# Expert weights fetched through two hardware queues instead of one, from block 56 on

## The chip, the cores and the metric

The program runs on one core of a Trainium2 chip. The metric is the device time in microseconds (us) of one execution. TensorE (PE) does the matrix products, VectorE (DVE) and ScalarE (ACT) the elementwise work, GpSimd (POOL) little here, and SyncE (SP) only issues transfers. A transfer that SyncE or ScalarE issues goes into that engine's own hardware queue; the queues are worked off by the core's 16 DMA engines.

## The reference, cut to what matters

Two transformer blocks run one after the other over 512 tokens of width 1024. The first ends in an expert layer: each of 16 experts takes its 64 best tokens, and everything is float32.

```
aff = softmax(h @ w_router); gate, idx = top_k(aff^T, 64)
xs = h[idx]                                          # per expert 64 x 1024
hid = silu(xs @ w_gate[e]) * (xs @ w_up[e])          # w_gate, w_up: 16 x 1024 x 2048
ys = (hid @ w_down[e]) * gate                        # w_down: 16 x 2048 x 1024
```

The three weights of the 16 experts are 403 MB of the 526 MB that the kernel reads.

## The kernel before, in words

The expert stage handles two experts at a time, in 8 passes p = 0 to 7. Expert 2p uses columns 0 to 63 of TensorE's array, expert 2p + 1 columns 64 to 127, so their matmuls alternate. The weights come in 192 blocks of 2048 KB, 24 to a pass. Block n has p = n // 24 and r = n % 24; even r is the even expert's, odd r the odd one's. r = 0 to 7 are the gate weights (four pairs), 8 to 15 the up weights, 16 to 23 the down weights. In what follows "pair m" is the blocks m and m + 1 with m even; TensorE starts on a pair when both blocks have landed (`landed_block`, line 1060).

In a pass TensorE does the four gate pairs (line 1075) with the combining of the pass before between them (line 1049), the four up pairs with the gathering of the next pass's tokens (line 1032), then the turning of h (`turn_h`, with VectorE's product of line 2448 and ScalarE's copies around it), and the four down pairs (line 1142).

From block 46 on there are 8 slots for weights in SBUF, and block n goes to the slot that block n - 8 had (`SLOT_OF`, `BEFORE`). `moe_used(BEFORE[n])` is the semaphore value that TensorE sets when it has used that block's pair. SyncE's program (`sync`) issues all blocks in order of n: for each it waits for `moe_used`, then issues line 540. The last four blocks, 188 to 191, are issued in halves and quarters (lines 543 and 548), so that the last matmuls wait for little.

ScalarE's loop over p (line 1722) does, for each pass: wait for the gate pairs, four Silu (line 1727); the four copies of hT; wait for the last down pair, two copies to ys.

Of the kernel before, what the change touches and what calls it, by code (L numbers as in the profile page):

```python
# [12 lines left out]
P = 128  # L13
# [31 lines left out]
def build_program(nc, I, out):  # L45
    ctx = ExitStack()
    with ctx:
        s = {n: ctx.enter_context(nc.semaphore("s_" + n)) for n in DMA_SEMS + SEMS}
# [5 lines left out]
        def up(ins, name, *key):  # L54
            ins.then_inc(s[name], 1)
            count[name] = at[(name, *key)] = at[name] = count.get(name, 0) + 1
# [4 lines left out]
        def val(name, *key):  # L61
            return at.get((name, *key) if key else name, 1) if counting else at[(name, *key) if key else name]
# [17 lines left out]
        def mem(n, at_=None):  # L80
            if at_ is None:
                at_ = cursor[0]
                cursor[0] += n
            assert at_ + n <= NW, (at_, n)
            assert at_ + n <= M or at_ >= M
            return low[:, at_:at_ + n] if at_ < M else high[:, at_ - M:at_ - M + n]
# [6 lines left out]
        def own(n, at_):  # L93
            if (at_, n) not in full:
                full[at_, n] = lay(f"f_{at_}_{n}", at_, n, F32)
            return full[at_, n][:, :]

        def v3(ap, a):
            return ap.rearrange("p (a b) -> p a b", a=a)

        def flat(ap):
            return ap.rearrange("p a b -> p (a b)")
# [72 lines left out]
        NBLK = 192  # L175
        HALVES = {10: (10, 11), 12: (12, 13), 14: (14, 16), 17: (17,), 18: (18, 19)}
        HALVED = [n for pair_ in HALVES.values() for n in pair_]
        moe_slot = [own(4096, a_) for a_ in (M + 20096, M + 24192, 0, 4096, M + 16000, 8192, 12288, XT_AT, M + 28288)]
        once_x, once_y, once_z = own(4096, M + 8704), own(3072, M + 12800), own(1024, M + 5120)
        turn_of = [8, 0, 1, 2, 3, 4, 5, 6, 7]  # L180
        SLOT_OF, FILLED, BEFORE, held = {}, {}, {}, {}
        for n in range(NBLK):
            if n in (7, 15):
                continue
            if n == 46:
                turn_of.remove(7)
            i = SLOT_OF[n] = turn_of[0]
            turn_of = turn_of[1:] + [i]
            BEFORE[n] = held.get(i)
            FILLED[n] = FILLED.get(held.get(i), 0) + (2 if n in HALVED else 1)  # L190
            held[i] = n
        ys = mem(1024, M + 12800)
        stm = v3(mem(2048, M + 13824), 4)
        sq2 = [mem(512, M + 24704), mem(512, M + 25216)]
# [237 lines left out]
        offk = [0, 512, 896, 1152]  # L432


        def sync(sp):
            def load_chunk(c):
                for i, (dst, src) in enumerate(chunks[c][0](whole(c))):
                    sp.dma_start(dst, src).then_inc(s[{ZF: f"zf{i}", CG: f"cg{i}"}.get(c, f"w{pair[c]}")], 16)
# [51 lines left out]
            sp.wait_ge(s[freed(N1 - 3)[0]], val(*freed(N1 - 3)))  # L490
            load_chunk(N1 - 1)

            def block(n):
                p, r = divmod(n, 24)
                e = 2 * p + r % 2
                if r < 16:
                    k = r % 8 // 2
                    src = I["w_up" if r > 7 else "w_gate"][0, e][256 * k:256 * k + 256, :]
                    return src.rearrange("(p r) n -> p (r n)", p=P)
                k = (r - 16) // 2  # L500
                return I["w_down"][0, e][512 * k:512 * k + 512, :].rearrange("(p r) n -> p (r n)", p=P)

            for n in (0, 1, 2, 15, *range(3, 15), *range(16, NBLK)):
                if n == 1:
                    sp.wait_ge(s["pe_inter"], val("pe_inter", 1, 3))
                    sp.wait_ge(s["a_fill"], val("a_fill"))
                    sp.wait_ge(s["v_fill"], val("v_fill"))
                    sp.wait_ge(s["g_y"], val("g_y"))
                    for i in range(2):
                        sp.dma_start(xres[:, 2 * i:2 * i + 2, :], x_v[:, 2 * i:2 * i + 2, :]).then_inc(s[f"x{i}"], 16)  # L510
                r, src = n % 24, block(n)
                k = (r - 16) // 2
                if n == 15:
                    sp.wait_ge(s["v_mix"], val("v_mix", "on", 3))
                    sp.wait_ge(s["pe_mix"], val("pe_mix", "xr", 3, 1))
                    sp.dma_start(once_x, src).then_inc(s["mx"], 16)
                    continue
                if n == 7:
                    sp.dma_start(once_y, src[:, 0:3072]).then_inc(s["my"], 16)
                    sp.dma_start(once_z, src[:, 3072:4096]).then_inc(s["my"], 16)  # L520
                    continue
                if n in HALVED:
                    for half, z in enumerate((slice(0, 2048), slice(2048, 4096))):
                        for m in HALVES.get(n, ()):
                            used = moe_used(BEFORE[m]) if half else half_used(BEFORE[m])
                            sp.wait_ge(s[used[0]], val(*used))
                            sp.dma_start(moe_slot[SLOT_OF[m]][:, z], block(m)[:, z]).then_inc(s[f"m{SLOT_OF[m]}"], 16)
                    continue
                i = SLOT_OF[n]
                if BEFORE[n] is not None:  # L530
                    used = moe_used(BEFORE[n])
                    sp.wait_ge(s[used[0]], val(*used))
                elif n == 9:
                    sp.wait_ge(s["pe_route"], val("pe_route", "h2", 3, 1))
                elif n == 3:
                    sp.wait_ge(s["pe_mix"], val("pe_mix", "res", 3))
                elif n == 5:
                    sp.wait_ge(s["pe_mix"], val("pe_mix", "res", 7))
                if n < NBLK - 4:
                    sp.dma_start(moe_slot[i], src).then_inc(s[f"m{i}"], 16)  # L540
                    continue

                sp.dma_start(moe_slot[i][:, 0:2048], src[:, 0:2048]).then_inc(s[f"m{i}"], 16)
                if r % 2:
                    for name, c0, c1 in (("mg", 2048, 4096),) if k == 2 else (("mh", 2048, 3072), ("mq", 3072, 4096)):
                        for e_ in range(2):
                            src = I["w_down"][0, 14 + e_][512 * k:512 * k + 512, :].rearrange("(p r) n -> p (r n)", p=P)
                            sp.dma_start(moe_slot[SLOT_OF[n - 1 + e_]][:, c0:c1], src[:, c0:c1]).then_inc(s[f"{name}{e_}"], 16)
# [21 lines left out]
        def half_used(n):  # L570
            return ("pe_half", n // 8, n % 8 // 2)

        def moe_used(n):

            p, r = divmod(n // 2, 12)
            return ("pe_down", p, r - 8) if r >= 8 else ("pe_up", p, r // 4, r % 4)
# [918 lines left out]
        def scalar(a):  # L1495
            def bank(*key):
                return banks[bank_of[key]] if key in bank_of else banks[0]

            def copy(o, i):
                return a.activation(o, i, ACT.Copy)  # L1500
# [194 lines left out]
            for t in range(4):  # L1695
                z = slice(128 * t, 128 * t + 128)
# [22 lines left out]
                                    scale=rtok[:, t:t + 1]), "a_route", "h2", t, half)  # L1719


            for p in range(8):
                a.wait_ge(s["pe_up"], val("pe_up", p, 0, 3))
                if p:
                    a.wait_ge(s["v_up"], val("v_up", p - 1, 3))
                for fc in range(4):
                    up(a.activation(stm[:, fc, :], bank("up", p, 0, fc)[:, :], ACT.Silu), "a_up", p, fc)  # L1727
                if p:
                    a.wait_ge(s["pe_down"], val("pe_down", p - 1, 3))
                if p == 1:  # L1730
                    for j in range(8):
                        a.wait_ge(s["pe_back"], val("pe_back", j))
                        up(copy(XT[:, j, :], bank("back", j)[:, :]), "xt_back", j)
                for fc in range(4):
                    a.wait_ge(s["pe_up"], val("pe_up", "h", p, fc))
                    up(copy(flat(hT[:, 4 * fc:4 * fc + 4, :]), bank("hT", p, fc)[:, :]), "hT", p, fc)
                a.wait_ge(s["pe_down"], val("pe_down", p, 3))
                if p:
                    a.wait_ge(s["pe_comb"], val("pe_comb", p - 1, 7))
                if p == 7:  # L1740
                    up(copy(ys[:, 0:128], bank("y", p, 0)[:, 0:128]), "ys", p, "first")
                    up(copy(ys[:, 128:512], bank("y", p, 0)[:, 128:512]), "ys", p, 0)
                    continue
                for f in range(2):
                    up(copy(ys[:, 512 * f:512 * f + 512], bank("y", p, f)[:, :]), "ys", p, f)
# [1242 lines left out]
        counting = False  # L2988
        block = ctx.enter_context(nc.Block())
        block.sync(sync)  # L2990
        block.scalar(scalar)
        block.vector(vector)
        block.gpsimd(gpsimd)
# [26 lines left out]
```

## Time and profile before

| | |
|---|---|
| median of 3 runs | 2102.88 us (2102.07 to 2102.92) |
| profiled execution | 2102.45 us |
| its span, first to last instruction | 2100.7 us |
| TensorE busy | 2007.0 us (96%) |
| VectorE, ScalarE busy | 907.5 us, 577.4 us |
| DMA | 529.60 MB, mean 252 GB/s |
| expert stage | about 394 to 1302 us of the span |

The profile's page gives busy time by engine, the span in 40 slices of 52.5 us, and the chain of waits that ended last. TensorE's busy time includes time in which it runs at less than its peak, so 96% does not say by itself that TensorE bounds every stage; the slices of DMA and the chain have to be read with it.

### The profile page before, as it was taken

To read this page: it belongs to the slowest core of one execution; us is meant where nothing else is said; L and a number is where in the kernel's file an instruction comes from. 1 tells how busy PE (TensorE), PEld (TensorE's weight loads), DVE (VectorE), ACT (ScalarE), POOL (GpSimd) and SP (SyncE) were. 2 spreads that over 40 slices of the span, in tenths; PEclk is the share of its full clock that TensorE was granted. 3 is DMA by queue.
4 is the path that set the end of the run, shared out by engine and by line. 5 is a ranking of instruction groups with operands and counts; after the bars stand their busy time and mean duration, and the time that the engine had idled before them with its cause. 6 is when DMAs were issued, how large, how long until landed. Compare 5 with 4: busy or idle time off the path is not lost.

```text
span 2100.7 us, 23813 instructions
## 1 busy us (share of the span) xinstructions
PE 2007.0 (96%) x9908; PEld 1254.4 (60%) x9908; DVE 907.5 (43%) x1489; ACT 577.4 (27%) x901; POOL 59.0 (3%) x107
## 2 busy tenths in 40 slices
PE   7999999999999999999999889999999999999998
PEld 5888777543533333242423324776788888888886
DVE  4666673320111111111101002777897566666555
ACT  5434323100100000000000001438635343344445
POOL 1000010000000000000000000005200000000000
PEclk9999999999999999999999999999999999999999
DMA  9462117898999999999999998142122322323222
GB/s 350 160 236 85 41 67 295 353 404 371 431 430 430 431 430 430 432 430 431 430 431 430 431 431 363 63 121 41 67 94 81 131 80 95 106 80 111 81 97 84
DMA packets 109228, 529.60 MB, mean 252 GB/s; under 512 B 15189, under 2 KB 43969, under 8 KB 83137
## 3 DMA queue, kind: packets, MB, share of 16 engines
q1 hardware_dynamic: 109121, 528.07, 62.3%
q8 instruction: 80, 1.31, 0.2%
q14 instruction: 27, 0.22, 0.0%
HBM read 525.95 MB, written 2.10 MB: 251 GB/s over the span
## 4 chain that ended last, share of the span: by engine, by line
PE 86%; DMA 7%; DVE 4%; issue 2%; ACT 1%; SPq 0%; POOL 0%; ACTq 0%; DVEq 0%
PE bank L1075 22%; PE bank L640 14%; PE bank L642 14%; PE bank L641 14%; DMA f<-in_w_gate_dram 6%; PE bank L1142 6%; PE bank L1032 3%; PE bank L1049 3%; PE bank L651 2%; PE bank L1241 1%; PE bank L1350 1%; DMA f<-in_w_in_dram 1%; DMA high<-in_x_dram 1%; PE bank L867 1%; DVE r L407 0%
## 5 line engine op out<-in xcount | busy, mean ns | idle before, releaser
L1075 PE MATMUL bank<-f,high 128*64 128x512 f32 x2048 | 473.1, 610 | 36.8 <-issue 18.1
L640 PE MATMUL bank<-r 128*128 128x512 f32 (+1 forms) x984 | 388.7, 395 | 3.4 <-DVE r L2084 2.7
L641 PE MATMUL bank<-r 128*128 128x512 f32 (+1 forms) x984 | 384.0, 390 | 0.0
L642 PE MATMUL bank<-r 128*128 128x512 f32 (+1 forms) x984 | 384.0, 390 | 0.0
L1075 PEld LDWEIGHTS bank<-f,high 128*64 128x64 f32 x2048 | 150.4, 139 | 328.7 <-issue 313.6
L1142 PE MATMUL bank<-f,high 128*64 128x512 f32 x1024 | 227.7, 603 | 7.7 <-issue 7.6
L1500 ACT ACTIVATE high<-bank 128x512 f32<-128x512 f32 (+3 forms) x97 | 53.2, 579 | 636.0 <-PE bank L651 296.8
L2419 DVE SCALAR_TENSOR_TENSOR f<-bank,low,f 128x512 f32<-128x512 f32 x64 | 48.0, 750 | 398.6 <-PE bank L1049 398.1
L640 PEld LDWEIGHTS bank<-r 128*128 128x128 f32 (+1 forms) x984 | 184.5, 187 | 48.4 <-issue 5.8
L642 PEld LDWEIGHTS bank<-r 128*128 128x128 f32 (+1 forms) x984 | 184.4, 187 | 40.0
L641 PEld LDWEIGHTS bank<-r 128*128 128x128 f32 (+1 forms) x984 | 184.5, 188 | 39.0 <-issue 0.7
L407 DVE TENSOR_TENSOR r<-f,r 128x1024 fp32r<-128x1024 f32 (+3 forms) x171 | 193.5, 1184 | 31.9 <-ACT r L401 31.8
L401 ACT ACTIVATE r<-f 128x1024 fp32r<-128x1024 f32 (+3 forms) x172 | 163.6, 1016 | 24.8 <-DMA f<-in_w_in_dram 10.2
L1142 PEld LDWEIGHTS bank<-f,high 128*64 128x64 f32 x1024 | 76.0, 139 | 153.5 <-issue 153.5
L640 PE MATMUL bank<-r,r 128*128 128x512 f32 (+1 forms) x400 | 150.2, 375 | 0.0
L642 PE MATMUL bank<-r,r 128*128 128x512 f32 (+1 forms) x400 | 149.0, 372 | 0.0
L641 PE MATMUL bank<-r,r 128*128 128x512 f32 (+1 forms) x400 | 148.9, 372 | 0.0
L2405 DVE TENSOR_SCALAR high<-bank,low 128x128 f32<-128x128 f32 x64 | 25.6, 406 | 279.0 <-PE bank L1032 279.0
L1727 ACT ACTIVATE high<-bank 128x512 f32<-128x512 f32 x32 | 16.5, 602 | 296.3 <-PE bank L1075 296.3
L640 PEld LDWEIGHTS bank<-r,r 128*128 128x128 f32 x400 | 75.4, 188 | 15.8 <-issue 2.0
L642 PEld LDWEIGHTS bank<-r,r 128*128 128x128 f32 x400 | 75.4, 188 | 13.2
L641 PEld LDWEIGHTS bank<-r,r 128*128 128x128 f32 x400 | 75.4, 189 | 12.8
(377 smaller groups left out, 1798.7 us busy)
## 6 DMA issues: line engine op xcount, KB each, us to landing
f<-in_w_gate_dram SPq DMA_DIRECT2D x63, 2048.0 KB, 23.4
f<-in_w_down_dram SPq DMA_DIRECT2D x60, 2048.0 KB, 26.3
f<-in_w_up_dram SPq DMA_DIRECT2D x59, 2048.0 KB, 25.6
f<-in_w_up_dram SPq DMA_DIRECT2D x32, 1024.0 KB, 7.3
f<-in_w_in_dram SPq DMA_DIRECT2D x13, 2048.0 KB, 7.7
high<-in_w_ada_dram SPq DMA_DIRECT2D x32, 512.0 KB, 5.4
f<-in_w_down_dram SPq DMA_DIRECT2D x14, 1024.0 KB, 10.5
f<-in_w_ada_dram SPq DMA_DIRECT2D x4, 2048.0 KB, 14.6
```

What stands on the lines that cost most here:

```text
L401: up(a.activation(high_part(c)[:, z], whole(c)[:, z], ACT.Copy), "hi", c, i)
L407: up(v.tensor_tensor(low_part(c)[:, z], whole(c)[:, z], high_part(c)[:, z].bitcast(F32), ALU.subtract), "lo_v", c, i)
L640: pe.matmul(o, wh, xh, start=first, stop=False)
L641: pe.matmul(o, wl, xh, start=False, stop=False)
L642: return pe.matmul(o, wh, xl, start=False, stop=last)
L651: ins = pe.transpose(o[:, m * n:m * n + m] if k == P else o[:, k * n:k * n + k], b, ident[0:k, 0:k])
L1032: ins = pe.matmul(o, H2[:, t, 256 * (k // 2) + k % 2:256 * (k // 2) + 256:2], Sp[i][:, t, :], start=t == 0, stop=t == 3)
L1049: up(pe.matmul(o[:, :], ys[:, 128 * d:128 * d + 128], SgT[p % 2], start=True, stop=True), "pe_comb", p, d)
L1075: ins = pe.matmul(o[64 * e:64 * e + 64, :], xsT[p % 2][:, 2 * k + r, 64 * e:64 * e + 64], ws[e](2048 * r + 512 * fc), start=k == 0 and r = ...
L1142: ins = pe.matmul(o[f][64 * e:64 * e + 64, :], hT[:, 4 * k + r, 64 * e:64 * e + 64], ws[e](1024 * r + 512 * f), start=k + r == 0, stop=k = ...
L1500: return a.activation(o, i, ACT.Copy)
L2419: up(v.scalar_tensor_tensor(out=XT[:, d, :], in0=bank("cb", p, d)[:, :], scalar=adaT[:, 40 + d, 0:1], in1=XT[:, d, :], op0=ALU.mult, op1=A ...
```

## The change

From block 56 on, the odd blocks up to 187 are issued by ScalarE; the even ones, and the blocks 188 to 191, stay with SyncE. ScalarE issues them in `refills(p, r0)`, called at three places of a pass, each time for the slots that the pairs of the next part free. The waits are the same values of the same semaphores.

```diff
--- before.py
+++ after.py
@@ -189,6 +189,10 @@
             BEFORE[n] = held.get(i)
             FILLED[n] = FILLED.get(held.get(i), 0) + (2 if n in HALVED else 1)
             held[i] = n
+        by_act = {}
+        for n in range(56, NBLK - 4):
+            if n % 2:
+                by_act.setdefault(BEFORE[n], []).append(n)
         ys = mem(1024, M + 12800)
         stm = v3(mem(2048, M + 13824), 4)
         sq2 = [mem(512, M + 24704), mem(512, M + 25216)]
@@ -432,6 +436,16 @@
         offk = [0, 512, 896, 1152]
 
 
+        def expert_block(n):
+            p, r = divmod(n, 24)
+            e = 2 * p + r % 2
+            if r < 16:
+                k = r % 8 // 2
+                src = I["w_up" if r > 7 else "w_gate"][0, e][256 * k:256 * k + 256, :]
+                return src.rearrange("(p r) n -> p (r n)", p=P)
+            k = (r - 16) // 2
+            return I["w_down"][0, e][512 * k:512 * k + 512, :].rearrange("(p r) n -> p (r n)", p=P)
+
         def sync(sp):
             def load_chunk(c):
                 for i, (dst, src) in enumerate(chunks[c][0](whole(c))):
@@ -490,16 +504,6 @@
             sp.wait_ge(s[freed(N1 - 3)[0]], val(*freed(N1 - 3)))
             load_chunk(N1 - 1)
 
-            def block(n):
-                p, r = divmod(n, 24)
-                e = 2 * p + r % 2
-                if r < 16:
-                    k = r % 8 // 2
-                    src = I["w_up" if r > 7 else "w_gate"][0, e][256 * k:256 * k + 256, :]
-                    return src.rearrange("(p r) n -> p (r n)", p=P)
-                k = (r - 16) // 2
-                return I["w_down"][0, e][512 * k:512 * k + 512, :].rearrange("(p r) n -> p (r n)", p=P)
-
             for n in (0, 1, 2, 15, *range(3, 15), *range(16, NBLK)):
                 if n == 1:
                     sp.wait_ge(s["pe_inter"], val("pe_inter", 1, 3))
@@ -508,7 +512,7 @@
                     sp.wait_ge(s["g_y"], val("g_y"))
                     for i in range(2):
                         sp.dma_start(xres[:, 2 * i:2 * i + 2, :], x_v[:, 2 * i:2 * i + 2, :]).then_inc(s[f"x{i}"], 16)
-                r, src = n % 24, block(n)
+                r, src = n % 24, expert_block(n)
                 k = (r - 16) // 2
                 if n == 15:
                     sp.wait_ge(s["v_mix"], val("v_mix", "on", 3))
@@ -519,12 +523,14 @@
                     sp.dma_start(once_y, src[:, 0:3072]).then_inc(s["my"], 16)
                     sp.dma_start(once_z, src[:, 3072:4096]).then_inc(s["my"], 16)
                     continue
+                if n > 55 and n % 2 and n < NBLK - 4:
+                    continue
                 if n in HALVED:
                     for half, z in enumerate((slice(0, 2048), slice(2048, 4096))):
                         for m in HALVES.get(n, ()):
                             used = moe_used(BEFORE[m]) if half else half_used(BEFORE[m])
                             sp.wait_ge(s[used[0]], val(*used))
-                            sp.dma_start(moe_slot[SLOT_OF[m]][:, z], block(m)[:, z]).then_inc(s[f"m{SLOT_OF[m]}"], 16)
+                            sp.dma_start(moe_slot[SLOT_OF[m]][:, z], expert_block(m)[:, z]).then_inc(s[f"m{SLOT_OF[m]}"], 16)
                     continue
                 i = SLOT_OF[n]
                 if BEFORE[n] is not None:
@@ -1719,12 +1725,21 @@
                                     scale=rtok[:, t:t + 1]), "a_route", "h2", t, half)
 
 
+            def refills(p, r0):
+                for r in range(r0, r0 + 8):
+                    for n in by_act.get(24 * p + r, ()):
+                        used = moe_used(BEFORE[n])
+                        a.wait_ge(s[used[0]], val(*used))
+                        a.dma_start(moe_slot[SLOT_OF[n]], expert_block(n)).then_inc(s[f"m{SLOT_OF[n]}"], 16)
+
             for p in range(8):
+                refills(p, 0)
                 a.wait_ge(s["pe_up"], val("pe_up", p, 0, 3))
                 if p:
                     a.wait_ge(s["v_up"], val("v_up", p - 1, 3))
                 for fc in range(4):
                     up(a.activation(stm[:, fc, :], bank("up", p, 0, fc)[:, :], ACT.Silu), "a_up", p, fc)
+                refills(p, 8)
                 if p:
                     a.wait_ge(s["pe_down"], val("pe_down", p - 1, 3))
                 if p == 1:
@@ -1734,6 +1749,7 @@
                 for fc in range(4):
                     a.wait_ge(s["pe_up"], val("pe_up", "h", p, fc))
                     up(copy(flat(hT[:, 4 * fc:4 * fc + 4, :]), bank("hT", p, fc)[:, :]), "hT", p, fc)
+                refills(p, 16)
                 a.wait_ge(s["pe_down"], val("pe_down", p, 3))
                 if p:
                     a.wait_ge(s["pe_comb"], val("pe_comb", p - 1, 7))
```

On SyncE, where the up weights of pass 2 are issued (blocks 56 on; the number behind f_ is the slot's place, and 44928 stands for block 55), the kernel before has:

```order
L540 DMA f_44928_4096<-in_w_gate_dram 128x4096 [waits s_pe_down]
L540 DMA f_49024_4096<-in_w_up_dram 128x4096 [waits s_pe_up]
L540 DMA f_0_4096<-in_w_up_dram 128x4096 [waits s_pe_up]
L540 DMA f_4096_4096<-in_w_up_dram 128x4096 [waits s_pe_up]
L540 DMA f_40832_4096<-in_w_up_dram 128x4096 [waits s_pe_up]
L540 DMA f_8192_4096<-in_w_up_dram 128x4096 [waits s_pe_up]
L540 DMA f_12288_4096<-in_w_up_dram 128x4096 [waits s_pe_up]
L540 DMA f_53120_4096<-in_w_up_dram 128x4096 [waits s_pe_up]
```

and the changed kernel has:

```order
L546 DMA f_44928_4096<-in_w_gate_dram 128x4096 [waits s_pe_down]
L546 DMA f_49024_4096<-in_w_up_dram 128x4096 [waits s_pe_up]
L546 DMA f_4096_4096<-in_w_up_dram 128x4096 [waits s_pe_up]
L546 DMA f_8192_4096<-in_w_up_dram 128x4096 [waits s_pe_up]
L546 DMA f_53120_4096<-in_w_up_dram 128x4096 [waits s_pe_up]
```

The rows with slots 0, 40832, 12288 and 44928 behind block 55, the odd blocks, are gone from SyncE; an even block now follows an even block.

On ScalarE, the kernel before has around passes 2 and 3 (L1500 are copies to hT and ys, L1727 the Silu):

```order
L1500 ACTIVATE high<-bank 128x512 [waits s_pe_comb,s_pe_down]
L1500 ACTIVATE high<-bank 128x512
L1727 ACTIVATE high<-bank 128x512 [waits s_v_up,s_pe_up]
L1727 ACTIVATE high<-bank 128x512 x3
L1500 ACTIVATE high<-bank 128x512 [waits s_pe_up,s_pe_down]
L1500 ACTIVATE high<-bank 128x512 [waits s_pe_up] x3
L1500 ACTIVATE high<-bank 128x512 [waits s_pe_comb,s_pe_down]
L1500 ACTIVATE high<-bank 128x512
```

and the changed kernel has (L1506 and L1741 are the same copies and Silu, L1733 the new transfers):

```order
L1506 ACTIVATE high<-bank 128x512 [waits s_pe_comb,s_pe_down]
L1506 ACTIVATE high<-bank 128x512
L1733 DMA f_4096<-in_w_up_dram 128x4096 [waits s_pe_up] x4
L1741 ACTIVATE high<-bank 128x512 [waits s_v_up,s_pe_up]
L1741 ACTIVATE high<-bank 128x512 x3
L1733 DMA f_4096<-in_w_down_dram 128x4096 [waits s_pe_up] x4
L1506 ACTIVATE high<-bank 128x512 [waits s_pe_up,s_pe_down]
L1506 ACTIVATE high<-bank 128x512 [waits s_pe_up] x3
L1733 DMA f_4096<-in_w_gate_dram 128x4096 [waits s_pe_down] x4
L1506 ACTIVATE high<-bank 128x512 [waits s_pe_comb,s_pe_down]
L1506 ACTIVATE high<-bank 128x512
```

Four transfers, each behind its own wait for TensorE, now stand ahead of the Silu, ahead of the hT copies and ahead of the ys copies of each pass.

## Rows read from the trace of the kernel before

**Rows 1.** Page, the span in 40 slices, GB/s moved by DMA
```profile
GB/s 350 160 236 85 41 67 295 353 404 371 431 430 430 431 430 430 432 430 431 430 431 430 431 431 363 63 121 41 67 94 81 131 80 95 106 80 111 81 97 84
```

**Rows 2.** Stretches: us, busy us (count) of each engine, TensorE clock, DMA share, GB/s
```profile
700.00:818.00 118.00, 110.30 (x506) 42.02 (x504) 14.65 (x23) 5.33 (x10) 0.00 (x0) 0.99 1.01 431
```

**Rows 3.** Chain of waits, whole span: start us, us, what
```profile
814.10 25.03 DMA f<-in_w_gate_dram
839.37 3.65 PE bank L1075 x16
...
1192.11 5.13 PE bank L1075 x16
```

**Rows 4.** Timeline of TensorE, 606 to 663: start us, us, instructions
```profile
613.86 3.65 PE L1075 MATMUL bank<-f,high 128*64 128x512 f32 x16 [1.00 <-DVE high L2412]
...
641.70 3.65 PE L1075 MATMUL bank<-f,high 128*64 128x512 f32 x16
```

**Rows 5.** Timeline of TensorE, 690 to 830
```profile
692.83 27.69 PE L1142 MATMUL bank<-f,high 128*64 128x512 f32 x128
```

**Rows 6.** What SyncE waited for, 393 to 1306: us in total, times, longest
```profile
SPq L540 <- PE bank L1075: 488.4, 57, 14.4
```

**Rows 7.** Issues of line 540, 610 to 612: ns min/median/max, first and last start
```profile
L540 SPq DMA_DIRECT2D f<-in_w_gate_dram x2: 328/380/432, 610.5 to 610.9; - x2
...
DMA to landing us min/median/max: 18.0/20.3/22.5
```

**Rows 8.** Issues of line 540, 622 to 623
```profile
L540 SPq DMA_DIRECT2D f<-in_w_up_dram x2: 328/380/432, 622.2 to 622.6; - x2
...
DMA to landing us min/median/max: 16.1/18.3/20.6
```

**Rows 9.** Issues of line 540, 1111 to 1112.3
```profile
L540 SPq DMA_DIRECT2D f<-in_w_up_dram x2: 328/380/432, 1111.5 to 1111.8; - x2
...
DMA to landing us min/median/max: 25.6/27.9/30.1
```

**Rows 10.** Issues of line 548, the last pieces of the last blocks
```profile
L548 SPq DMA_DIRECT2D f<-in_w_down_dram x6: 432/1354/5403, 1259.6 to 1278.2; - x6
...
DMA to landing us min/median/max: 21.1/27.4/29.2
```

**Rows 11.** Chain of waits, last up pair and first down pair, passes 4 and 6
```profile
908.45 7.02 PE bank L1075 x32
...
925.11 7.04 PE bank L1142 x32
...
1143.24 7.02 PE bank L1075 x32
...
1158.36 7.04 PE bank L1142 x32
```

**Rows 12.** Issues of line 540, 1229.5 to 1230.5
```profile
L540 SPq DMA_DIRECT2D f<-in_w_up_dram x2: 327/379/431, 1229.8 to 1230.1; - x2
...
DMA to landing us min/median/max: 25.2/27.5/29.7
```

**Rows 13.** Timeline of TensorE, 1160 to 1310, the end of the stage
```profile
1259.92 7.09 PE L1075 MATMUL bank<-f,high 128*64 128x512 f32 x32 [1.18 <-issue]
...
1271.92 21.66 PE L1142 MATMUL bank<-f,high 128*64 128x512 f32 x96
1294.43 7.09 PE L1142 MATMUL bank<-f,high 128*64 128x512 f32 x32 [0.84 <-issue]
1302.08 2.81 PE L1049 MATMUL bank<-high 128*128 128x512 f32 x6 [0.57 <-ACT high L1500]
```

**Rows 14.** DMA, 708 to 712: packets, MB, share of 16 engines
```profile
q8 instruction: 1, 0.02, 1.4%
```

**Rows 15.** Issues of line 540, 684.5 to 685.5
```profile
L540 SPq DMA_DIRECT2D f<-in_w_down_dram x2: 327/380/432, 684.8 to 685.2; - x2
...
DMA to landing us min/median/max: 21.5/24.4/27.3
```

## The prediction, made before the changed kernel ran

> **What bounds the kernel now.** I read the page's slices first: from slice 11 to slice 24 the core moves a flat 430 GB/s [rows 1]. Then the stretches by engine: in one expert pass of 118 us ScalarE is busy 5.3 us, TensorE 110 us, and the 16 DMA engines are full (share 1.01) at 431 GB/s [rows 2]. A block is 2048 KB, 2.097 MB, so it costs 2.097/431 = 4.87 us, a pair (one block of the even expert, one of the odd) 9.74 us, a pass of 12 pairs 116.9 us. The chain of waits agrees: it goes back from the first gate matmuls of a pass to a weight transfer of 25 us, and from 839.37 to 1192.11 three passes take 352.7 us, 117.6 each [rows 3]. TensorE alone needs less: in pass 2 the gate pairs follow each other every 9.28 us ((641.70 - 613.86) / 3), the four down pairs take 27.69 us without a gap, and the whole pass, from 613.86 to 692.83 + 27.69 = 720.5, takes 106.7 us [rows 4, 5]. So the stage is bound by the bytes, with 10 us of TensorE slack in a pass. The sync engine is not late: it waits 488 us in 57 waits for TensorE to free a slot [rows 6], and a block lands 16 to 30 us after its issue [rows 7, 8, 9], so three to six blocks are always in flight. An earlier or quicker issue is worth nothing here. What can matter is the order in which bytes arrive, and the rate.
>
> **The change, part by part.** *Issues.* 66 of SyncE's transfers go to ScalarE. An issue takes 0.33 to 0.43 us on SyncE [rows 7]; I take the same on ScalarE. Each waits for a TensorE step that ScalarE's next real work (Silu, copies of hT, copies of ys) waits for anyway, so only the last of each four stands ahead of that work: 0.4 us before Silu, before the hT copies (VectorE must multiply first) and before the ys copies (used after the first gate pair of the next pass). ScalarE's 112 idle us of a pass hide it; uncovered it would be 3 x 0.4 us a pass, 7 us in all. In pass 7's end no ScalarE issue is left, since block 187 goes when pair 178 is used. I take 0.
>
> *Bytes.* The same bytes through the same 16 engines: 0 on the total. As long as either queue holds work the engines stay full; SyncE's keeps three even blocks outstanding, 14.6 us at full rate. The last quarter was issued at 1278.2 and landed 21.1 us later, at 1299.3 [rows 10]; I expect that landing unmoved.
>
> *Order.* This is where time goes. In one queue a pair lands together. With two queues that share evenly, an odd block issued into an empty queue moves at half rate at once and lands 9.74 us later, though it is needed much later; the even blocks wait behind their backlog at half rate. At 622.6, when block 57 is issued, blocks 54 and 55 are due at 628.6 and 633.4 (610.5 + 18.0, 610.9 + 22.5) and 56 at 638.3 (622.2 + 16.1) [rows 7, 8]. So SyncE's queue has 15.7 us of work up to block 56, 31.4 us at half rate: 654.0. Block 57 lands at 632.3. The odd lead, d, is 21.7 us.
>
> How much of d survives? Odd block m+9 enters the slot freed when pair m is used, at free(m), and at half rate lands 9.74 later. It belongs to a pair whose even block lands 4 x 9.74 = 38.96 after even block m. Hence d is at most 38.96 - 9.74 - (free(m) - landing(m)) = 29.2 - (free - landing). When a wait breaks this, ScalarE's queue runs empty, the even blocks get the full rate, and d shrinks; nothing makes it grow again. The latest free is that of the first down pair, behind the turning of h. The last up pair was issued at 1111.8, landed 30.1 later at 1141.9 and began at 1143.2, 1.3 late [rows 9, 11]. The down pair began 15.1 us after it, in pass 4 16.7 [rows 11], and its weights land 9.74 after the up pair's: it begins 6.7 to 8.3 after landing and is used 7.0 later. So free - landing is 13.7 to 15.3 and d is 15.5 to 13.9. As d only shrinks, the latest counts: 13.9.
>
> When an even block lands, the odd ones are d/9.74 blocks further than in order, so that many blocks' time (4.87 each) has gone to bytes not yet wanted: TensorE runs d/2 = 7.0 us behind the kernel before, from pass 2 or 3 to pass 7. This is a constant lag, not a loss per pass, and it would cost nothing if TensorE could make it up at the end.
>
> *The end.* It can't. Before, pair 182 landed at 1230.1 + 29.7 = 1259.8 and began at 1259.92 [rows 12, 13]. After: 1266.9. From there TensorE needs 12.0 us to the first down pair (1259.92 to 1271.92) and then 27.7 us for the four down pairs where no weight is late [rows 5, 13]: 1306.6. The remaining weights are all in by 1299.3, so none stops it. Before, the last pair ran from 1294.43 to 1301.5 [rows 13], 2.2 us behind the last landing. Difference 5.1 us. Behind it TensorE goes straight on with the combining (1302.08), so nothing later takes it back; SyncE's next weights are issued as TensorE frees slots and have DMA engines that now fall idle earlier.
>
> Sum: 0 + 0 + 5.1. Span 2100.7 + 5.1 = 2105.8; the profiled execution took 2102.45, and the median of the runs, 2102.88, stands 0.43 above it. Predicted 2108.0. With d at 15.5 it is +5.9; if the last shrinking overshoots to 12, +4.1; with lost TensorE clock at the end up to +7. Own range of this case 2106.5 to 2110.5.
>
> On sharing, one rule is worth its place: the Trainium skill, DMA: Bandwidth & Descriptors, section Queues, rings and completion order, says each DMA engine round-robins between the queues that have work, packet by packet. By it the lag above follows; were queues served by age of issue there would be none, and the sum would be 0. The trace has instruction fetches of a second queue (q8) in the middle of the full stretch [rows 14], but not when they were issued, so it doesn't settle the shares.
>
> **Rivals.** *A: no change.* The engines serve the two queues nearly in order of issue, or SyncE's deeper queue gets more than half, so d is small; below 4.2 us of lag at the end the result can't be told from no change. For it: the same bytes, the same engines, a stage bound by bytes alone. Against: nothing in the program ties an odd block to its even partner. 2102.9 to 2107. The skill's same page, section Issuing engines are not separate DMA queues, says that issuing on several engines saves only issue time; by that rule the time stays at 2102.9, and nothing waits for an issue here.
>
> *B: faster.* Two queues hide what one leaves. Three passes took 117.6 us each against 116.9 at 431 GB/s: 0.7 us a pass, and a landing came 6.1 us behind the one before it (684.8 + 21.5, 685.2 + 27.3) where 4.87 is normal, with a fetch between [rows 14, 15]. If that went, the 5.8 passes after 622 give 4.1 us, and the 431 itself may hide as much again: 4 to 8 us, 2095 to 2099 without a lag. It decides only from a gain of 0.9 us a pass on, where 5.8 passes outweigh the lag's 5.1 us. Against: share 1.01 leaves no idle time to fill.
>
> *C: a lower rate.* Switching between queues costs an engine time. That late landing bounds it: 6.1 - 4.87 = 1.2 us, less 0.6 for the fetch's own 16 KB at 27 GB/s an engine, is 0.6 us for a switch out and back. A pair gives each engine 8 rows of 16 KB from each queue, so 8 x 0.6 = 4.8 us on 9.74; 66 pairs: 320 us, time 2420. The other bound is 0. The fetch goes to another kind of memory, and the share stays 1.01 around it, so I take 0, but 5% of that is already 16 us. The skill's section Latency and other measured facts (same page) gives 103 GB/s for 128 rows at a pitch of 8 MiB, the distance between an even and an odd expert here; by it this case would be worse still, but only two such streams run here, and no run shows it.
>
> **Chances.** Forecast 0.50, A 0.26, B 0.10, C 0.14. What a measurement of this kernel can tell from no change is 0.2%, 4.2 us. Faster 0.10 (B). Same: A and 0.05 of the forecast, 0.31. Slower: 0.45 + 0.14 = 0.59. The range takes in the forecast, A, half of B and the small end of C, and leaves out 0.15: 2098 to 2115.
>
> **What would show it.** Right: DMA share and GB/s unchanged in the full stretch; issue to landing near 10 us on ScalarE and near 30 or more on SyncE; TensorE's pass starts 6 to 8 us later than before from pass 3 on and the same distance in pass 6; the last down pair ending near 1306.6 with few waits in the down stage. A would show pass starts within 2 us. C would show GB/s below 425 and passes longer than 118. Wrong above all: an uneven share of the two queues, which moves d directly.

## The result, and the profile after

| | before | changed |
|---|---|---|
| median of 18 runs each | 2102.93 us | 2106.68 us |
| ratio, 95% interval | | 1.0015 (1.0008 to 1.0021) |
| span of the profiled execution | 2100.7 us | 2104.6 us |

The change makes the kernel slower by 1.7 to 4.4 us by the ratio, 3.2 in the middle (the two medians lie 3.75 us apart). The middle is below the 0.2%, 4.2 us, that the prediction took as its bound for telling a change from none. I had said 2108.0 us, 5.1 us more than before, for the reason that the runs bear out, with one of its terms too large.

The page of the changed kernel, the line with the GB/s of the 40 slices and its queues (q1 is SyncE's, q10 the new one, ScalarE's: packets, MB, share of the 16 engines):

```profile
GB/s 350 160 238 82 41 67 294 354 401 374 430 431 430 431 429 432 431 430 431 430 431 430 431 431 348 63 120 41 58 103 80 130 81 91 110 80 111 80 97 84
...
q1 hardware_dynamic: 99617, 389.65, 46.8%
q10 hardware_dynamic: 9504, 138.42, 15.4%
```

The plateau is the one of [rows 1]: 430 GB/s with one queue, 430 with two. 138 MB have moved to the second queue and nothing has become faster or slower by it. The stretches by engine show the same for one pass, against [rows 2]:

```profile
700.00:818.00 118.00, 108.00 (x488) 41.34 (x486) 14.73 (x23) 5.33 (x10) 0.00 (x0) 0.97 1.01 431
```

ScalarE's busy time in the pass is unchanged too. The new thing is in the issues. Here are the two that end the old order, at 622.9 (block 56 on SyncE, line 546, then block 57 on ScalarE, line 1733), the same two lines for pair 182, and the pieces that land last (line 554); under each, the time from issue to landing:

```profile
L546 SPq DMA_DIRECT2D f<-in_w_up_dram x1: 328/328/328, 622.9 to 622.9; - x1
...
DMA to landing us min/median/max: 28.1/28.1/28.1
...
L1733 ACTq DMA_DIRECT2D f<-in_w_up_dram x1: 391/391/391, 622.9 to 622.9; - x1
...
DMA to landing us min/median/max: 14.9/14.9/14.9
...
L546 SPq DMA_DIRECT2D f<-in_w_up_dram x1: 328/328/328, 1236.4 to 1236.4; - x1
...
DMA to landing us min/median/max: 29.6/29.6/29.6
...
L1733 ACTq DMA_DIRECT2D f<-in_w_up_dram x1: 361/361/361, 1236.4 to 1236.4; - x1
...
DMA to landing us min/median/max: 19.5/19.5/19.5
...
L554 SPq DMA_DIRECT2D f<-in_w_down_dram x6: 432/839/2694, 1266.0 to 1278.5; - x6
...
DMA to landing us min/median/max: 21.2/22.3/23.3
```

Block 56 landed at 651.0 and block 57 at 637.8: the odd lead d, the landing of a pair's even block less that of its odd block, is 13.2 us. At pair 182 it is 29.6 - 19.5 = 10.1 us. In [rows 7, 8, 12] both blocks of a pair land one block's time apart, the even one first. The last piece landed at 1278.5 + 21.2 = 1299.7, in [rows 10] at 1299.3: the bytes end where they did.

TensorE's timeline shows the first gate pair of passes 4 and 7 and the end of the stage:

```profile
845.36 3.65 PE L1081 MATMUL bank<-f,high 128*64 128x512 f32 x16 [2.98 <-DMA f<-in_w_gate_dram]
...
1197.81 2.83 PE L1081 MATMUL bank<-f,high 128*64 128x512 f32 x6 [3.93 <-DMA f<-in_w_gate_dram]
...
1266.05 7.09 PE L1081 MATMUL bank<-f,high 128*64 128x512 f32 x32 [0.93 <-DMA f<-in_w_up_dram]
...
1277.62 27.69 PE L1148 MATMUL bank<-f,high 128*64 128x512 f32 x128
1305.89 2.38 PE L1055 MATMUL bank<-high 128*128 128x512 f32 x5 [0.58 <-ACT high L1506]
```

Pass 4 starts at 845.36 where [rows 3] have 839.37, pass 7 at 1197.81 where they have 1192.11: 6.0 us late and 5.7 us late, a constant lag over three passes (passes 3, 5 and 6 start 5.7, 5.7 and 6.0 us late). Pair 182 starts at 1266.05 against 1259.92 in [rows 13], 6.1 us late. Then the four down pairs run through in 27.69 us without a wait, and the last ends at 1305.3 instead of 1301.5, 3.8 us late, 5.6 us behind the last landing instead of 2.2.

### The profile page after: what moved, and what is told of

It reads as the page before. It is cut to its first block, busy times and chain, and to the rows that moved or that the text cites. A ratio compares the mean times of both kernels' runs of the same rounds, so it can differ in the third digit from the quotient of the medians.

```text
span 2104.6 us, 23813 instructions
## 1 busy us (share of the span) xinstructions
PE 2003.5 (95%) x9908; PEld 1248.2 (59%) x9908; DVE 908.1 (43%) x1489; ACT 577.1 (27%) x901; POOL 58.7 (3%) x107
## 4 chain that ended last, share of the span: by engine, by line
PE 75%; DMA 20%; DVE 3%; issue 1%; ACT 1%; SPq 0%; POOL 0%; ACTq 0%; DVEq 0%
PE bank L646 14%; PE bank L648 14%; PE bank L647 14%; PE bank L1081 14%; DMA f<-in_w_up_dram 9%; DMA f<-in_w_gate_dram 7%; PE bank L1148 6%; DMA f<-in_w_down_dram 3%; PE bank L1055 2%; PE bank L657 2%; PE bank L1038 2%; PE bank L1247 1%; PE bank L1356 1%; DMA f<-in_w_in_dram 1%; DMA high<-in_x_dram 1%
## 5 line engine op out<-in xcount | busy, mean ns | idle before, releaser
L1081 PEld LDWEIGHTS bank<-f,high 128*64 128x64 f32 x2048 | 144.9, 139 | 336.6 <-issue 289.6
L1148 PE MATMUL bank<-f,high 128*64 128x512 f32 x1024 | 225.1, 597 | 10.3 <-DMA f<-in_w_down_dram 10.1
L1506 ACT ACTIVATE high<-bank 128x512 f32<-128x512 f32 (+3 forms) x97 | 53.2, 579 | 635.3 <-PE bank L657 294.4
L405 ACT ACTIVATE r<-f 128x1024 fp32r<-128x1024 f32 (+3 forms) x172 | 163.6, 1016 | 26.1 <-DMA f<-in_w_in_dram 11.2
L1148 PEld LDWEIGHTS bank<-f,high 128*64 128x64 f32 x1024 | 72.3, 138 | 157.1 <-issue 140.6
L1741 ACT ACTIVATE high<-bank 128x512 f32<-128x512 f32 x32 | 16.5, 603 | 299.7 <-PE bank L1081 299.7
```

What stands on the lines that cost most here:

```text
L405: up(a.activation(high_part(c)[:, z], whole(c)[:, z], ACT.Copy), "hi", c, i)
L1081: ins = pe.matmul(o[64 * e:64 * e + 64, :], xsT[p % 2][:, 2 * k + r, 64 * e:64 * e + 64], ws[e](2048 * r + 512 * fc), start=k == 0 and r = ...
L1148: ins = pe.matmul(o[f][64 * e:64 * e + 64, :], hT[:, 4 * k + r, 64 * e:64 * e + 64], ws[e](1024 * r + 512 * f), start=k + r == 0, stop=k = ...
```

## The experiments

Two theories stood against each other. **L**, the lag: the queue that starts empty beside a full one gets half the engines at once and leads; TensorE waits for the other queue's block with d/2 of the engines' time already spent on blocks not yet wanted; only what it can't make up behind the last pairs counts. **I**, a price per block on ScalarE's queue, or **F**, a fixed price of a second queue. In the diffs, which are cut to the lines that matter, ON_ACT is the list of blocks that ScalarE issues; in the changed kernel it is the odd ones from 57 to 187.

The profiled executions start this stage at times up to 3 us apart (the first gate matmul at 395.5 to 398.6), for reasons ahead of it, so each profile is read against its own last landing. From the start of the first down pair to that landing pass 827.2 to 827.7 us in all kernels of the table but e7, where it is 830.5; e5 is not in the table. "Head" is from the start of pair 182 to the last landing, "tail" from there to the end of the last down pair. The tail's excess over the 2.2 us of before is what the lag costs.

| | d at pair 182 | head | tail | tail - 2.2 | ratio, as us (95%) |
|---|---|---|---|---|---|
| before | (one queue) | 39.4 | 2.2 | 0 | 0 |
| changed | 10.1 | 33.7 | 5.6 | 3.4 | +3.2 (1.7 to 4.4) |
| e1_from_20 | -5.4 | 36.0 | 4.7 | 2.5 | +1.5 (-0.4 to 3.4) |
| e2_until_143 | (one queue) | 39.0 | 2.3 | 0.1 | -0.2 (-1.9 to 1.7) |
| e3_from_150 | 11.6 | 33.0 | 6.2 | 4.0 | +4.0 (2.1 to 5.9) |
| e4_one_later | -4.8 | 37.0 | 2.2 | 0 | +0.6 (-1.1 to 2.5) |
| e6_even_on_act | -9.5 | 34.2 | 5.1 | 2.9 | +1.9 (0.0 to 3.8) |
| e7_sync_in_halves | 18.8 | 30.1 | 10.8 | 8.6 | +8.6 (5.7 to 11.4) |

The last column is the ratio less 1, times the 2104 us of the kernel before beside it. It agrees with the column to its left within 1 us in every row, though in e7 not for the whole of the cost (see there). A d of -4.8 us in two queues is not the 4.9 us by which the even block lands first in one queue: there the pair's bytes come one block behind the other, while two queues that share evenly have moved half a block of the next pair by the time the odd one lands.

**e1_from_20.** Both queues start at block 20, at 446.7, when SyncE's queue holds only one block more, due 1.7 us later.

```diff
-        for n in range(56, NBLK - 4):
-            if n % 2:
-                by_act.setdefault(BEFORE[n], []).append(n)
+        ON_ACT = [n for n in range(20, 188) if n % 2 == 1]
+        for n in ON_ACT:
+            by_act.setdefault(BEFORE[n], []).append(n)
```

> ScalarE takes the odd blocks from 20 on, 84 of them instead of 66, and both queues start when the DMA engines have nothing in flight. Theory L (the slowdown is half of the lead that ScalarE's queue won by starting empty beside a full one): no lead arises, odd and even blocks of a pair land within 3 us of each other, and the time is that of the kernel before within 1.5 us. Rival I (each block on ScalarE's queue costs something, 3.8 us for 66): plus 4.8 us. Rival F (a fixed cost of having a second queue): plus 3.8 us.

Ratio 1.0007 (0.9998 to 1.0016). No odd lead arose, but the even blocks lead by 5.4 us (issued together at 1233.5, landed 24.6 and 30.0 later), so "within 3 us" was wrong, and the time lies between L and the rivals. The pairs started as L says, within 0.2 us up to the one issued at 559.9; from the next on the even block leads by 4 to 8 us. What starts this is not shown. That even lead is worth half of it, 2.7 us, less what the end makes up; in this profile the tail also holds slower matmuls: the four down pairs take 28.65 us instead of 27.69. By itself e1 excludes I (+4.8) and, with an interval that ends at 3.4, just excludes F (+3.8).

**e2_until_143.** ScalarE's blocks end at 143.

```diff
+        ON_ACT = [n for n in range(56, 144) if n % 2 == 1]
```

> ScalarE takes the odd blocks 57 to 143 only, 44 of them; from 144 on all go through SyncE as before. L: passes 3 to 5 start 5 to 6 us later than in the kernel before, the lead is gone once ScalarE's last block is used, and the end is within 1 us of the kernel before. I: plus 2.5 us. F: plus 3.8 us.

Ratio 0.9999 (0.9991 to 1.0008). L holds: 44 blocks cost nothing. TensorE's timeline of this kernel, the starts of passes 4 and 6, pair 182 and the last down pair, and its last pieces:

```profile
846.34 1.08 PE L1081 MATMUL bank<-f,high 128*64 128x512 f32 x4 [1.47 <-DMA f<-in_w_gate_dram]
...
1076.75 1.51 PE L1081 MATMUL bank<-f,high 128*64 128x512 f32 x6 [1.41 <-DMA f<-in_w_gate_dram]
...
1262.83 8.65 PE L1081 MATMUL bank<-f,high 128*64 128x512 f32 x32 [2.64 <-issue]
...
1296.98 7.09 PE L1148 MATMUL bank<-f,high 128*64 128x512 f32 x32 [0.21 <-issue]
...
L554 SPq DMA_DIRECT2D f<-in_w_down_dram x6: 431/1537/3644, 1261.1 to 1279.6; - x6
...
DMA to landing us min/median/max: 22.2/26.2/30.4
```

The last piece landed at 1301.8, so this execution's bytes ended 2.5 us later than in [rows 10], and the last pair ended at 1304.1, 2.3 us behind it, as before. Less those 2.5 us, TensorE was 4.5 us late at the start of pass 4 (846.34 against 839.37) and 4.7 at those of passes 3 and 5, a little under the 5 to 6 expected, and not late at all at the start of pass 6, where the chain of the kernel before has:

```profile
1074.17 1.90 PE bank L1075 x7
```

**e3_from_150.** ScalarE takes only the last 19.

```diff
+        ON_ACT = [n for n in range(150, 188) if n % 2 == 1]
```

> ScalarE takes only the odd blocks 151 to 187, 19 of them. L: the lead arises at once and stands at some 10 us at pair 182, so the time is plus 3 to 5 us, as with all 66. I: plus 1.1 us. F: plus 3.8 us, but then e1 and e2 show it too.

Ratio 1.0019 (1.0010 to 1.0028): 19 blocks cost as much as 66. With e2 this decides between the theories: 44 early blocks cost nothing and 19 late ones the whole. It also bears on what sets the size of d. Block 151, issued at 1073.8 beside a deeper backlog than block 57, led by 23.1 us (landed 14.1 us after its issue, block 150 37.3), but two pairs on the lead was 12.9: as the prediction's bound has it, the slots' coming free decides what is left, not how far the first block led. The timeline and both landings of pair 182:

```profile
1266.95 7.09 PE L1081 MATMUL bank<-f,high 128*64 128x512 f32 x32 [0.93 <-DMA f<-in_w_up_dram]
1278.52 27.69 PE L1148 MATMUL bank<-f,high 128*64 128x512 f32 x128
...
L546 SPq DMA_DIRECT2D f<-in_w_up_dram x1: 328/328/328, 1236.5 to 1236.5; - x1
...
DMA to landing us min/median/max: 30.4/30.4/30.4
...
L1733 ACTq DMA_DIRECT2D f<-in_w_up_dram x1: 362/362/362, 1236.5 to 1236.5; - x1
...
DMA to landing us min/median/max: 18.8/18.8/18.8
```

**e4_one_later.** ScalarE waits one pair longer with each block.

```diff
-            by_act.setdefault(BEFORE[n], []).append(n)
+            by_act.setdefault(BEFORE[n] + 2, []).append(n)
...
-                        used = moe_used(BEFORE[n])
+                        used = moe_used(BEFORE[n] + 2)
```

> As the change, 66 blocks, but ScalarE issues each one pair later (it waits for the use of pair m+2 where block m+9 takes the slot of pair m). L: the lead can be at most 38.96 - 9.74 - 15.9 (issue to landing from an empty queue, as measured after the change) - (use - landing), 5 us behind ordinary pairs and about 0 behind the turning of h; so it falls to about 0 and the time is that of the kernel before within 1.5 us. I and F: plus 3.8 us.

Ratio 1.0003 (0.9995 to 1.0012), as L said; I and F, at +3.8 us, lie outside its interval of -1.1 to 2.5. The lead is not 0 but -4.8 us: even blocks land 25.1 us after their issue at 1235.3, the odd one 20.9 us after 1244.3. The half of that, 2.4 us, is just what the end makes up.

**e5_two_later.** The same with two pairs (`+ 4`).

> As the change, but ScalarE issues each block two pairs later. L: now the odd blocks are the late ones; the lead can be at most 38.96 - 19.48 - 15.9 - (8.4 to 12.6), that is -4.8 to -9 us, TensorE waits for odd blocks, and half of it, 2.4 to 4.5 us, is the lag at pair 182; TensorE makes up 2.3 us of a lag at the end, so the time is plus 0 to 2.2 us. I and F: plus 3.8 us.

Ratio 1.0581 (1.0554 to 1.0609), plus 122 us: the expectation fell. One stretch of it, the share of DMA at the end, and the issue of one odd block:

```profile
818.00:935.00 117.00, 96.04 (x408) 36.34 (x410) 13.83 (x21) 5.33 (x10) 0.00 (x0) 0.91 0.89 363
...
L1733 ACTq DMA_DIRECT2D f<-in_w_gate_dram x1: 361/361/361, 742.3 to 742.3; - x1
...
DMA to landing us min/median/max: 14.0/14.0/14.0
```

The engines are no longer full. An odd block is issued when a pair is used, lands 14.0 us later, and is needed two pairs on: two pairs take 8.3 (the use) + 14.0 = 22.3 us, 11.2 each, where the bytes need 9.74. The 363 GB/s of this stretch make it 9.74 x 431 / 363 = 11.6 us a pair, and 66 times the 1.8 us between is 120 us, nearly the whole of the loss. The bound that I used says how far the lead can fall, not that the queue can keep its pace below it. By the 11.2 us it would be 96 us over 66 pairs; the rest I put on the slower stretches of TensorE after each wait (granted clock 0.91 here, 0.99 in [rows 2]) without having measured it apart.

**e6_even_on_act.** The mirror image: the even blocks on ScalarE.

```diff
+        ON_ACT = [n for n in range(56, 188) if n % 2 == 0]
```

> The mirror of the change: from block 56 on the even blocks (to 186) go to ScalarE and the odd ones stay with SyncE. L: now the even ones lead by some 10 us, since it is the queue that starts empty that gets ahead, and the time is plus 3 to 4.5 us. A theory in which it matters which of the two blocks of a pair is early has no reason for the same number.

Ratio 1.0009 (1.0000 to 1.0018), below the 3 to 4.5 us that I had named, though its interval reaches 3.8. The lead is the mirror's, -9.5 us (the even block of pair 182 on ScalarE and the odd one on SyncE are issued together; the rounded rows give 9.6), and in the profile the end is 2.9 us further behind the last landing:

```profile
L1733 ACTq DMA_DIRECT2D f<-in_w_up_dram x1: 362/362/362, 1236.8 to 1236.8; - x1
...
DMA to landing us min/median/max: 21.2/21.2/21.2
...
L546 SPq DMA_DIRECT2D f<-in_w_up_dram x1: 327/327/327, 1236.8 to 1236.8; - x1
...
DMA to landing us min/median/max: 30.8/30.8/30.8
```

That the empty queue leads, whichever blocks it carries, is shown; the size is the least sure of the table.

**e7_sync_in_halves.** The change, but SyncE's blocks from 48 on go as two column halves, so its rows are 8 KB and ScalarE's 16 KB.

```diff
-                    sp.dma_start(moe_slot[i], src).then_inc(s[f"m{i}"], 16)
+                    if n > 47:
+                        sp.dma_start(moe_slot[i][:, 0:2048], src[:, 0:2048]).then_inc(s[f"m{i}"], 16)
+                        sp.dma_start(moe_slot[i][:, 2048:4096], src[:, 2048:4096]).then_inc(s[f"m{i}"], 16)
```

> As the change, but from block 48 on SyncE issues its blocks as two column halves, so that its rows are 8 KB where ScalarE's stay 16 KB. If the DMA engines take turns row by row, ScalarE's queue (q10) moves two thirds of the bytes while both have work, its first block takes 3.5 + 1 us until all engines have it and 7.3 us more, 12 us from issue to landing instead of 14.9, and the lead grows: plus 4 to 6 us. If they share by bytes, the lead and the time are those of the change, plus 3.8 us. If the 3.5 us between an issue into an empty second queue and its first packet is a number of rows of the other queue taken in advance, it halves to about 1.8 us; if it is a time, it stays 3.5.

Ratio 1.0041 (1.0027 to 1.0054), plus 8.6 us: turns row by row, and more than the 4 to 6 us I had worked out. The lead is 18.8 us. The view of the DMA queues, first the changed kernel from 640 to 660, then e7 from 626 to 628 (packets, MB, share):

```profile
q1 hardware_dynamic: 297, 4.33, 50.5%
q10 hardware_dynamic: 295, 4.31, 50.3%
```

```profile
q10 hardware_dynamic: 35, 0.57, 66.8%
q1 hardware_dynamic: 35, 0.29, 33.8%
```

In both the packets are equal in number: 297 to 295 and 35 to 35. In the first the bytes are equal too; in e7 ScalarE's are twice SyncE's. This makes the lead larger, and the time with it.

The 8.6 us of the table's two columns agree more closely than the evidence allows. The shorter rows also lower the plateau, which the table leaves out:

```profile
1052.00:1170.00 118.00, 108.45 (x499) 42.84 (x499) 15.74 (x25) 5.36 (x11) 0.00 (x0) 0.97 1.00 425
...
1271.67 8.78 PE L1085 MATMUL bank<-f,high 128*64 128x512 f32 x32 [2.05 <-DMA f<-in_w_up_dram]
```

The changed kernel has 431 GB/s in that stretch, and from the first down pair to the last landing e7 takes 3.0 us more than the kernel before. With them the stage of this profile is 11.6 us longer, just above the interval of the ratio, which rests on four runs. Pair 182 took 8.78 us here at a granted clock of 0.83 and 7.09 in the changed kernel; so of the lag of 9.3 us (head) only 0.7 was made up. e7 shows that the lead and the time grow with it; how much of the 8.6 us is the lead's is less sure.

## Why the prediction was right, point by point

*What bounds the stage.* Right. DMA share 1.01 and 430 GB/s before and after, and the last landing moved 0.4 us.

*Issues: 0.* Right. An issue takes 0.36 us on ScalarE (0.36 to 0.39 in the rows above), and e2 puts 44 of them there for nothing.

*Rates: 0.* Right, and rival C is out: two queues taking turns move 431 GB/s in a pass, as one does. In the Trainium skill, DMA: Bandwidth & Descriptors, the section Queues, rings and completion order gives turns by the packet; e7's 35 to 35 packets agree. The page's packet holds typically 9 to 17 descriptors, while a packet of the profile is here one row of 16 or 8 KB. The drop to 103 GB/s that the same page gives, in its section Latency and other measured facts, for 128 rows at a pitch of 8 MiB does not appear with two streams 8 MiB apart (431 GB/s).

*Order.* Right in kind: the odd blocks lead, TensorE is late by a constant 6.0 and 5.7 us in passes 4 and 7, and rival A is out in both its forms: the engines do not serve by age, and SyncE's deeper queue does not get more than its half (297 to 295 packets). Mis-sized was the sentence that an odd block issued into an empty queue "moves at half rate at once and lands 9.74 us later". Block 57 took 14.9 us, and the sign "near 10 us on ScalarE" failed: its 66 blocks land 14.9 to 23.1 us after their issue. In the stretch behind its issue the view of the queues has SyncE's alone, and only then both:

```profile
q1 hardware_dynamic: 95, 1.46, 97.2%
```

```profile
q10 hardware_dynamic: 33, 0.54, 63.0%
q1 hardware_dynamic: 29, 0.36, 42.2%
```

The first is 622.8 to 626.3, the second 626.3 to 628.3. So the lead began at 13.2 us, not 21.7: block 57 landed 5.5 us later than worked out (637.8 for 632.3), and block 56, whose queue kept all the engines for those 3.5 us, 3.0 us sooner (651.0 for 654.0). The first of the two stands in the bound on d as well, where I had 9.74 us from issue to landing. Block 73 was issued at 702.4, when ScalarE's queue was nearly empty, and landed 15.9 us later; pair 64, whose use freed its slot, had landed at 659.7 + 30.1 = 689.8. So d can be at most 38.96 - 15.9 - (702.4 - 689.8) = 10.5 us, where I had 15.5 to 13.9 (with 13.7 to 15.3 us for the bracket that is 12.6). Block 73 itself led by 9.5 us, and 10.1 was measured at the end.

*Half of d as lag.* Nearly right: 10.1 / 2 = 5.0, and the head shrank by 5.7 us (39.4 to 33.7). That the lag was 0.7 above the half is part of why the sum missed by only 1.7 us. Over the table the head shrinks by half of d, to within 0.7 us, whatever the sign of d.

*The end.* Right in kind: the down pairs are TensorE's own (27.69 us in one piece), and most of the lag stays. TensorE makes up 2.3 us (5.7 less 3.4), where my sum had 1.9. e2 and e3 show that nothing but this end counts. Both terms together, a lag of 5.7 where I had 7.0 and 2.3 where I had 1.9, make 3.4 instead of 5.1.

*Rival B, faster.* Out. The plateau did not rise.

## What to carry to other kernels

A transfer queue that is always backed up is not only a pipe but an order. Splitting it over two issuing engines left the rate here as it was (431 GB/s) and gave the order away: the queue with the shorter backlog gets blocks that nobody wants yet, and the consumer runs late by half of that lead. In the middle of a stage bound by bytes this cost nothing (e2); it is paid once, where the consumer itself becomes the bound behind the last blocks, so the last stretch should be issued in the order of use through one queue. Delaying the shorter queue's issues by one pair cured it here too (1.0003), but one pair more emptied the queue and cost 122 us.

## What the runs showed of the hardware that I had not expected

- A transfer issued into an empty second queue while the first has a backlog does not start at once. In the changed kernel block 57 is issued at 622.9 and up to 626.3 only q1 moves packets. In e7, where SyncE's rows are half as long, the issue was at 621.7, and the view of the queues from 621.7 to 625.1 has:

```profile
q1 hardware_dynamic: 195, 1.46, 101.4%
```

  Nothing of q10 here either. So some 3.4 us pass in both, with 95 packets of q1 in the one and 195 in the other: it is not a count of the other queue's rows. It is no fixed time either. In e1 ScalarE's first issue, at 446.7, found SyncE's queue nearly empty, as said, and q10 starts within 2 us. From 446.7 to 448.6 and from 448.6 to 450.6 the views have:

```profile
q1 hardware_dynamic: 45, 0.39, 73.8%
```

```profile
q10 hardware_dynamic: 29, 0.48, 57.5%
q1 hardware_dynamic: 21, 0.34, 40.0%
```

  e5's first issue, with 2.3 us of work left in SyncE's queue, took the same 1.9 us. So the wait depends on how much the other queue still holds; whether by a time or by an amount of bytes taken in advance (1.46 MB of q1 in both stretches), and why, stays open.
- The two queues share by rows and not by bytes (35 to 35 packets, 0.57 to 0.29 MB): whoever issues longer rows gets more of the bandwidth while both have work.
